# Expert units of a mixture layer: 128x128 transposes of rows taken from TensorE and made on VectorE in 32x32 blocks

## The reference, cut to what matters

```python
def expert(acc, xs):
    wg, wu, wd, ge = xs          # (1024, 256), (1024, 256), (256, 1024), gate of each token
    y = (jax.nn.silu(x @ wg) * (x @ wu)) @ wd
    return acc + ge[:, None] * y.astype(jnp.float32), None
```

## Time and profile before

| | |
|---|---|
| device time, three runs | 1518.1, 1521.2, 1524.0 us; median 1521.2 |
| span of the profiled execution | 1515.0 us, 21977 instructions |
| outside the span | not listed for the profiled execution itself; the median of the runs is 6.2 us longer than the span |
| TensorE's mean granted clock | 0.963 of 2.4 GHz |
| expert stage, first gate product to last y copy | 856.5 to 1440.1 us |

### The profile page before, as it was taken

One profiled execution on the slowest core, in us unless ns is written; L12 is line 12 of the kernel. 1 busy time (PEld: TensorE's weight loads), 2 busy tenths in 40 slices (PEclk: granted clock), 3 DMA queues, 4 the chain that ended last, 5 costly groups with the idle time before them and its releaser, 6 DMA issues. The chain is left out here.

```text
span 1515.0 us, 21977 instructions
## 1 busy us (share of the span) xinstructions
PE 1382.7 (91%) x8510; PEld 790.0 (52%) x8510; DVE 562.3 (37%) x1291; ACT 294.7 (19%) x677; POOL 314.4 (21%) x334
## 2 busy tenths in 40 slices
PE   5999999999979999899988799998999999999966
PEld 3876777764657777675444334443344343434322
DVE  2001465452724464455894334211121111111138
ACT  1002343443323321120121001111111111111021
POOL 6000000000079993000044111211111121111100
PEclk9999999999989999999999899999999999999988
DMA  9411310123464444674011989999999999999485
GB/s 338 172 56 39 111 58 0 70 71 112 137 183 141 137 139 115 240 258 166 35 43 49 399 348 411 401 416 415 421 395 403 409 421 400 406 402 421 188 314 226
DMA packets 106882, 358.50 MB, mean 237 GB/s; under 512 B 28915, under 2 KB 31091, under 8 KB 80659
## 3 DMA queue, kind: packets, MB, share of 16 engines
q1 hardware_dynamic: 81366, 301.98, 51.3%
q0 software_dynamic: 15968, 40.61, 7.3%
q10 hardware_dynamic: 9446, 14.51, 2.8%
HBM read 331.49 MB, written 38.15 MB: 244 GB/s over the span
## 5 line engine op out<-in xcount | busy, mean ns | idle before, releaser
L2132 PE MATMUL bank<-arena 128*32 128x512 f32 (+2 forms) x1536 | 338.1, 621 | 20.0 <-DMA arena<-in_w_up 19.2
L2132 PEld LDWEIGHTS bank<-arena 128*32 128x32 f32 (+2 forms) x1536 | 120.9, 139 | 204.8 <-issue 203.4
L2140 PE MATMUL bank<-arena 128*32 128x512 f32 (+2 forms) x768 | 168.6, 598 | 0.7 <-DVE arena L2886 0.7
L2119 POOL DMA_INDIRECT expert_rows<-arena x46 | 46.4, 1008 | 486.8 <-PE bank L2125 420.2
L2880 DVE TENSOR_TENSOR arena<-arena,bank 128x256 f32<-128x256 f32 x46 | 19.4, 421 | 324.1 <-ACT arena L2537 324.1
L1210 PE MATMUL bank<-arena 128*128 128x272 f32 x512 | 129.1, 405 | 0.7 <-ACT arena L1247 0.3
L438 PE MATMUL bank<-arena 128*128 128x272 f32 x480 | 113.9, 400 | 3.6 <-PEq L132 1.9
L2140 PEld LDWEIGHTS bank<-arena 128*32 128x32 f32 (+2 forms) x768 | 55.0, 134 | 110.3 <-issue 109.4
L1210 PEld LDWEIGHTS bank<-arena 128*128 128x128 f32 x512 | 96.0, 193 | 27.1 <-issue 6.1
L438 PEld LDWEIGHTS bank<-arena 128*128 128x128 f32 x480 | 93.0, 194 | 24.0 <-issue 2.8
L668 PE MATMUL bank<-arena 128*128 128x272 f32 x384 | 100.1, 405 | 0.0
(11 more groups left out here) (482 smaller groups left out, 1790.3 us busy)
## 6 DMA issues: line engine op xcount, KB each, us to landing
arena<-in_w_gate SPq DMA_DIRECT2D x64, 1024.0 KB
arena<-in_w_up SPq DMA_DIRECT2D x64, 1024.0 KB
arena<-in_w_down SPq DMA_DIRECT2D x64, 1024.0 KB, 15.2
arena<-in_w_ada SPq DMA_DIRECT2D x12, 2048.0 KB, 9.0
arena<-in_w_in SPq DMA_DIRECT2D x11, 2048.0 KB, 8.8
arena<-expert_rows SPq DMA_DIRECT2D x8, 2048.0 KB, 25.5
gate_logits<-arena ACTq DMA_DIRECT2D x16, 272.0 KB, 3.3
arena<-gate_logits SPq DMA_DIRECT2D x8, 544.0 KB, 5.0
```

The costliest lines, as they stand in the source:

```text
L2119: return nc.gpsimd.indirect_dma_start(out=y_d, out_offset=bass.IndirectOffsetOnAxis(ap=rows, axis=0), in_=of, in_offset=None, bounds_check ...
L2132: mm = nc.tensor.matmul(out[rows].rearrange("p (a n) -> p a n", a=2), x[:, k, rows], gate_up_slot(n)[:, :, k, :], start=k == 0, stop=k == ...
L2140: mm = nc.tensor.matmul(out[rows, :], h[:, k, rows], down_slot(n)[:, k, 512 * half:512 * half + 512], start=k == 0, stop=k == 1)
```

## The change

`xT` and `hiddenT` leave TensorE. VectorE makes both from SBUF to SBUF. A block transpose on VectorE handles 32x32 blocks inside 32 partitions, so each unit takes 16 instructions for `XT` (4 groups of 32 rows by 4 quarters of each 128 channels; one reads 32 partitions x 256 elements and writes 32 partitions x 256) and 16 for `hidT` (32 partitions x 64 elements each). The two 128-row PSUM copies of VectorE and the PSUM copy of ScalarE go away. ScalarE's silu waits for `hidT` of two units before, the gather of a unit waits for VectorE's `XT` of four units before. The order on VectorE becomes `xT(u+1)`, `hidden(u)`, `hiddenT(u)`, y copy of u-1.

```diff
             for u in range(NU):
-                if u:
-                    hiddenT(u - 1)
-                if u + 1 < NU:
-                    xT(u + 1)
                 gate_up_of(u)
...
-            xT_low(0)
             for u in range(NU):
-                if u + 1 < NU:
-                    xT_low(u + 1)
                 silu(u)
...
-            def xT_high(u):
-                dve.wait_ge(xt_mm.sem, 2 * u + 2)
+            def xT(u):
+                dve.wait_ge(g_ld[u % RX].sem, 16 * (u // RX + 1))
                 if u >= 2:
                     dve.wait_ge(gu_mm.sem, u - 1)
-                nc.vector.tensor_copy(XT[u % 2][:, 4:8, :], bank[1].ap().rearrange("p (k n) -> p k n", k=4)).then_inc(xt_v.sem, 1)
+                for a in range(4):
+                    slots = slice(QUAD * a, QUAD * a + QUAD)
+                    by_quarter = Xg[u % RX][slots].rearrange("p (k q j) -> p q k j", k=KD, q=4)
+                    for q in range(4):
+                        ins = nc.vector.transpose(XT[u % 2][QUAD * q:QUAD * q + QUAD, :, slots], by_quarter[:, q])
+                ins.then_inc(xt_v.sem, 1)
...
             def hiddenT(u):
-                dve.wait_ge(at_mm.sem, u + 1)
+                dve.wait_ge(a_done.sem, u + 1)
                 if u >= 2:
                     dve.wait_ge(d_mm.sem, u - 1)
-                nc.vector.tensor_copy(hidT[u % 2], bank[4][:, 0:2 * P].rearrange("p (k n) -> p k n", k=2)).then_inc(at_sb2.sem, 1)
+                for a in range(4):
+                    slots = slice(QUAD * a, QUAD * a + QUAD)
+                    by_quarter = hid[u % 2][slots].rearrange("p (q j k) -> p q k j", q=4, k=2)
+                    for q in range(4):
+                        ins = nc.vector.transpose(hidT[u % 2][QUAD * q:QUAD * q + QUAD, :, slots], by_quarter[:, q])
+                ins.then_inc(at_sb2.sem, 1)
...
-            xT_high(0)
+            xT(0)
             for u in range(NU):
-                if u:
-                    hiddenT(u - 1)
                 if u + 1 < NU:
-                    xT_high(u + 1)
+                    xT(u + 1)
                 hidden(u)
+                hiddenT(u)
```

More of the change, by code:

```diff
@@ L2098, in build @@
     y_out = [Tick(nc, f"rows_scattered{i}") for i in range(RY)]
-    xt_mm, xt_a, xt_v, gu_mm, silu_d, a_done, at_mm, at_sb2, d_mm, y_a, y_v = (Tick(nc, n) for n in (
-        "xT_in_psum", "xT_copied_low", "xT_copied_high", "gate_up_product", "silu_done", "hidden_done", "hiddenT_in_psum",
-        "hiddenT_copied", "down_product", "y_copied_low", "y_copied_high"))
+    xt_v, gu_mm, silu_d, a_done, at_sb2, d_mm, y_a, y_v = (Tick(nc, n) for n in (
+        "xT_made", "gate_up_product", "silu_done", "hidden_done", "hiddenT_made", "down_product", "y_copied_low", "y_copied_high"))
     l2_load, all_rows = Tick(nc, "ln2_loaded"), Tick(nc, "all_rows_written")
@@ L2361, in shared_step @@
                 sd_mm.inc(mm) if half else sd_low.inc(mm)
-            def xT(u):
-                pe.wait_ge(g_ld[u % RX].sem, 16 * (u // RX + 1))
-                for half, free in enumerate((xt_a, xt_v)):
-                    if u:
-                        pe.wait_ge(free.sem, u)
-                    transpose_rows(half, Xg[u % RX]).then_inc(xt_mm.sem, 1)
             def gate_up_of(u):
                 parts = UNITS[u][1]
-                pe.wait_ge(xt_a.sem, u + 1)
                 pe.wait_ge(xt_v.sem, u + 1)
@@ L2378, in gate_up_of @@
                 gate_up(bank[2 + u % 2], XT[u % 2], parts).then_inc(gu_mm.sem, 1)
-            def hiddenT(u):
-                pe.wait_ge(a_done.sem, u + 1)
-                if u:
[L2383 to L2386, removed]
             def down_of(u):
@@ L2399, in _ @@
             pe.wait_ge(s_hid.sem, NT)
-            xT(0)
             pe.wait_ge(s_fold.sem, 3)
             for u in range(NU):
-                if u:
-                    hiddenT(u - 1)
-                if u + 1 < NU:
-                    xT(u + 1)
                 gate_up_of(u)
@@ L2413, in _ @@
                     shared_step(*SHARED_BESIDE[u][1])
-            hiddenT(NU - 1)
             down_of(NU - 1)
@@ L2525, in _ @@
             shared_hiddenT(2)
[L2527 to L2531, removed]
             def silu(u):
@@ L2535, in silu @@
                 if u >= 2:
-                    act.wait_ge(at_mm.sem, u - 1)
+                    act.wait_ge(at_sb2.sem, u - 1)
                 nc.scalar.activation(hid[u % 2], bank[2 + u % 2][:, 0:FF], ACT.Silu).then_inc(silu_d.sem, 1)
@@ L2612, in gather @@
                 if u >= RX:
-                    pool.wait_ge(xt_mm.sem, 2 * (u - RX) + 2)
+                    pool.wait_ge(xt_v.sem, u - RX + 1)
                 col = UNITS[u][0]
```

## The result

The changed kernel takes 1545.6 us (median of 4 runs, 1543.6 to 1547.2) against 1522.6 us before: a ratio of 1.0149 with a 95% interval of 1.0125 to 1.0172. It is slower, as forecast and inside the range of 1520 to 1690. But 1593 was forecast, a loss of 72 us, and the loss is 23. The size was wrong by a factor of three. The profiled execution has a span of 1542.0 us.

The account below looks back on a forecast made before the run. TensorE and DMA were taken as close limits now, VectorE as the bound after. From 850.9, 46 turns of 13.7 (630), 23.9, 2.7 and 4.9 end at 1512.4, against 1440.1: 72.3 more, about 1593 us, range 1520 to 1690.

Parts of the forecast that it names:

- the forecast's signs: Expected in the changed profile: VectorE busy nearly all stage, TensorE waiting for `xT` and no longer weights, DMA well under 0.9.
- the turn of VectorE, 13.7 us: VectorE's work per unit: `xT` 7.39, `hiddenT` 4.99, `hidden` and y copy 1.11, hand-overs 0.2; above TensorE's 10.55 and DMA's 11.8.
- The 0.045 us for the stride: Added to each 64-element `hiddenT` transpose because `hid` is read with a stride of two words; lower bound nothing.
- the fill of 0.017: 17 ns added to each transpose, as a 32x32 block cannot leave before its last element is in; middle of 0 and 33.
- My lower bound of 12.4: VectorE's turn in us with all terms low (no fill, no stride, gap 0.035), giving a time of 1534.
- The formula: Time of the whole kernel in us as 963.5 + 46 x VectorE's turn.
- 7.6 (2.7, 1.3 and 3.6): VectorE's waits in us: 2.7 for silu at the start; at the end 1.3 for `hidden(45)`'s product, 3.6 for the last down.
- The sum of work in the first turns, 23.9 us: VectorE work formerly hidden in idle time, now added: fold pairs 5.8, sums of gates 3.55, values of gates 14.5.
- Overlap: Rival: VectorE's transposes pipeline like the MAX8, turn 9.6 us, up to 20 us won, about 1503; chance 0.09.
- half rate: Rival: a transposed 4-byte element takes two cycles on VectorE, turn 19.0 us, time 1838; chance 0.07.
- The clock: Rival: TensorE's idle 3 us a turn lowers its granted clock; whole turn at 1.2 GHz gives about 1930; chance 0.04.
- The worth of the removal: 20 us at the most: Gain from removing TensorE's transposes, limited by DMA: expert-stage transfers take 544 us at 419 GB/s instead of 564.

Follow-up runs that it names:

- full-height run: Changed kernel with four transposes of 128 partitions in place of each 16 of 32, blocks not moved between partition groups: 1513.9 us, 0.9940 of the kernel before.
- the run without stride: Changed kernel with `hid` read in contiguous runs of 32 words instead of every second word: 1549.7 us, a single time.
- the runs with one part alone: Changed kernel with `hiddenT` back on TensorE: 1519.4 us, 0.9981; kernel before with only `hidT` made on VectorE: 1521.2 us, 0.9979 (both ratios to the kernel before).

## Why the prediction was right and wrong

**The bound and its direction: right.** VectorE became the limit of the stage, because instructions that change their 32 partitions do not overlap. The full-height run shows the other case. But it is the limit alone only in the first seven turns; later it shares the pace with the transfers. So two of the forecast's signs did not come: DMA is busy 0.98 of units 7 to 44, not well under 0.9, and the gate product still waits for weights, 33.8 us of it:

```profile
PE bank L2131 <- DVE arena L2847: 40.8, 22, 4.6
PE bank L2131 <- DMA arena<-in_w_up: 33.8, 9, 5.6
```

**The step that failed is the turn of VectorE, 13.7 us, which is 12.39.** It is the mis-sized term; three surcharges in it were not there:

- `hiddenT`: 4.99 forecast, 16 x 0.250 = 4.0 measured. The 0.045 us for the stride is zero (the run without stride shows it), and the gap is 0.250 - 0.236 = 0.014, not 0.035. The row that I took for the stride was of a multiplication with its output walked 128 words apart, and I gave it to a transpose with a stride of two. The Trainium skill's 2.5 ns a column for small strides (Vector Engine (DVE) Microarchitecture Reference, Measured stream behaviour on trn2), taken there with a program of another kind and steps of 24 words, would have made it worse; the 236 ns either way show nothing of it.
- `xT`: 7.39 forecast, 7.18 measured. The duration is 0.436 where I had 0.427 with the fill of 0.017; the gap again 0.013.
- hand-overs 0.2 forecast, 0.13 measured (four of 0.03).

Together 1.3 us a turn, 60 us over 46 turns. My lower bound of 12.4 was the truth. A smaller slip beside it: the MAX8 rows' 0.071 us is the whole distance of two starts; beyond 8 columns of 1.04 ns it leaves 0.063. Taking the middle of bounds for terms that each occur 736 times made the error.

**The formula then gives 963.5 + 46 x 12.39 = 1533.4; the measured time is 12 higher.** The waits of VectorE in the stage of the changed kernel (total us, times, longest):

```profile
DVE arena L2853 <- ACT arena L2508: 11.1, 6, 3.1
...
DVE arena L2870 <- PE bank L2139: 3.1, 1, 3.1
DVE arena L2835 <- PE bank L2359: 2.8, 1, 2.8
```

These are 17.0 us, where I had counted 7.6 (2.7, 1.3 and 3.6). The 2.8 are for the shared expert's product in turn 2, which I had not seen. Of the 11.1, 3.1 stand at the start and 2.5 at the end; the other four, 5.5 us, lie in the later turns of 13 to 15 us, where the weights came late and the gate product behind the wait ran slower (see the rivals below). So "in the steady state VectorE waits for nobody" was right at 13.7 and fails now and then at 12.39, just under what the transfers allow. That explains 9.4 of the 12. The other 3 are not of the change. VectorE's list starts later, with the gather:

```profile
855.54 14.38 DVE L2847 STREAM_TRANSPOSE arena<-arena 32x256 f32<-32x256 f32 x32 [3.31 <-DMA arena<-h_rows,arena]
```

This is 4.6 us behind the 850.9 of the kernel before. The tail takes 75.7 us instead of 74.9. And the 6.2 us that I added were the distance of a median from the span of a single execution; here it is 1545.6 - 1542.0 = 3.6. So 4.6 + 0.8 - 2.6 = 2.8.

**Why the loss is so small: not said by any step as such.** At 13.7 my sum did not need it: the later turns would all have been VectorE's. At 12.39 they equal the transfers' 12.5, so the change is free there, and only the first turns pay. The sum of work in the first turns, 23.9 us, was the right term: moving the gates' part of it (18) took 18.1 us out of them.

**Rivals.** Overlap did not happen; half rate did not (1.04 ns an element, from 0.449 - 0.250 over 192). The clock mattered little: the mean granted clock went from 0.963 to 0.952, and in most turns TensorE had slack. Where it had waited for weights, the next gate product was slower. Two products of one shape in the changed kernel, and their stretches:

```profile
1403.36 8.78 PE L2131 MATMUL bank<-arena 128*64 128x512 f32 x32 [4.26 <-DMA arena<-in_w_up]
...
1426.06 7.04 PE L2131 MATMUL bank<-arena 128*64 128x512 f32 x32
```

```profile
1403.36:1412.14 8.78, 8.78 (x33) 3.20 (x33) 6.74 (x16) 0.00 (x0) 2.00 (x2) 0.81 1.02 421
1426.06:1433.10 7.04, 7.04 (x35) 2.23 (x31) 6.72 (x22) 0.58 (x1) 1.01 (x1) 1.00 0.95 381
```

The first, behind a wait of 4.26 us, ran at a mean granted clock of 0.81, so in part at the lower of the two levels (1.2 GHz), the second at 1.00 (2.4 GHz). VectorE waited 2.29 us in that turn, and 1.7 of it is this difference. In the four later turns with a wait the product took 8.6 to 9.7 us, so by my estimate up to 5 of their 5.5 us are the clock's, behind waits for weights.

**The worth of the removal: 20 us at the most was right as a bound, 9 as a fact.** The 20 us rested on 419 GB/s, read from one stretch of 10 us. Over units 7 to 44, in the kernel before and then at full height, the DMA engines were busy all the time at less:

```profile
953.55:1420.57 467.02, 446.98 (x2237) 184.87 (x2238) 78.96 (x149) 57.53 (x111) 72.47 (x72) 0.97 1.00 406
...
944.50:1414.02 469.52, 413.73 (x1867) 145.65 (x1868) 113.38 (x371) 35.83 (x74) 72.42 (x72) 0.94 1.00 408
```

So the transfers were already the limit of these turns before the change. At 408 GB/s the 227.8 MB take 558 us, an estimate 6 below the 564 and not 20. This fits the runs with one part alone and at full height, which all came out above what I expected of them.

## What to carry to other kernels

Before pricing a shift of work from one engine to another, find the pace of the third party: here the weights need about 12.5 us a turn on the average, so a turn of 10.6, 11.8 or 12.4 costs about the same, and one of 13.4 costs its full excess. Take that pace from a long stretch, not from the best 10 us. A price that is multiplied by 1472 must be taken from the nearest row without surcharges for mechanisms that no row of that instruction shows; keep them for the range. And look at the turns in which the receiving engine has other work: they, not the steady ones, may carry the whole loss.

## What the hardware showed that I had not expected

Transposes of 4-byte elements in 32x32 blocks grow by 1.04 ns for each element of a partition. One of 256 elements lasts 0.436 us, where the `hidden` operation of 256 lasts 0.42, and one of 64 lasts 0.236, where an operation of 64 on two inputs lasts 0.225, so there is no visible fill beyond 0.02 us. Reading every second word cost nothing (0.236 us either way). Queued transposes on the same partitions begin 0.333 us apart for 256 elements and 0.136 for 64, those that write other partitions each time 0.449 and 0.250: about 0.115 us for each change of the 32 partitions. Cutting such an instruction in two on the same partitions costs only 0.061 us. Whether a change of the partitions that are read would be enough to keep two apart was not tested: here the written ones change every time.
